# Entry to the first stage, set-up transfers, order of the modulation vectors and the compressed branch of a two-block transformer kernel

## Chip, cores and metric

The kernel runs on one core of one Trainium2 chip. The metric is the device time of one execution in microseconds (us), as the median of several runs. The core has a matrix engine (TensorE, PE in the rows; PEld is its weight load), a vector engine (DVE), a scalar engine (ACT), GpSimd (POOL) and SyncE, whose queue (SP) issues nearly all transfers.

## Reference

Two transformer blocks, each with two layers, run one after the other over 256 tokens of width 1024, all in float32. The first block's layer is feed-forward, mixing (retention, block attention, convolution), feed-forward. The second block's layer has the same shape with a modulation, computed from one vector `c`:

```
cond = silu(c)
for l in range(2):
    mod = cond @ ada_w[l] + ada_b[l]          # 9 vectors of 1024
    sh1, sc1, ga1, sh2, sc2, ga2, sh3, sc3, ga3 = split(mod, 9)
    n = rms_norm(h) * (1 + sc1) + sh1 ; h = h + 0.5 * ga1 * swiglu(n)
    n = rms_norm(h) * (1 + sc2) + sh2 ; h = h + ga2 * token_mixing(n)
    n = rms_norm(h) * (1 + sc3) + sh3 ; h = h + 0.5 * ga3 * swiglu(n)
```

Inside `token_mixing` one of three attentions has a compressed branch: 15 overlapping windows of 32 keys (and of 32 values) are each flattened and sent through a small two-layer network.

```
def compress(t, j):                            # j = 0 keys, 1 values
    blk = t[:, cmp_idx] + cmp_pe[j]            # 15 windows x 32 x 64
    hid = silu(blk.reshape(15, 2048) @ cmp_w1[j])   # 128 wide
    return hid @ cmp_w2[j]
```

## The kernel before

The program is twelve stages in a row (`SUBS`): f1, m, f2 twice for the first block, F1, M, F2 twice for the second. The same Python class hierarchy is played once per engine, so every engine's instructions are written in one common order; semaphores do the rest.

**Weights.** All weights stream from memory in units of up to 1 MB through four buffers `raw`. A unit is cut into subs of two 128-row tiles of 512 columns. For each sub ACT writes a rounded copy `wh` (`split_hi`, L2021) and DVE the remainder `wl` (`split_lo`, L2292); PE then does three matmuls per tile and half of the tokens: `xh*wh`, `xh*wl`, `xl*wh` (`sub`, L1713, L1714, L1716), twelve in a full sub. There are five `wh`/`wl` buffers, and `ahead` keeps the splits three subs in front of PE in feed-forward stages. SyncE issues the load of a buffer's next unit behind the remainder of its last sub (`load`, L2747).

**Entry.** `enter` turns `x` (2 x 128 tokens by 1024) with sixteen PE transposes (L1688) into banks 6 and 7: eight, then eight more in the same two banks once ACT (`xh`, L2048) and DVE (`xl`, L2339) have read the first eight. Only behind all of this come the first three weight splits (`ahead`), and behind them the four squares of the norm (L2041).

**Set-up.** Behind the first four weight loads SyncE issues 18 transfers of constants: the large part of `cst` (1.7 MB), convolution weights, embeddings, positions, `w2d`, `lngb`. In the second column chunk of the first stage (`c == 1`), right behind `turn_h(0)`, `setup_rest` has PE turn three small tiles one behind the other, and DVE and ACT compute the rotary angles.

**Modulation.** The 36 vectors of 512 columns (`q`; 72 half units of weights) are summed by DVE: one multiply-add over 128 x 512 per weight tile (`mac`, L2300), four to a half unit. `ADA_BY` says how many half units are placed by the end of each stage from the fourth on. When a vector is whole, ACT and DVE split it (`ach`, `acl`), PE sums it over the partitions with two matmuls (`sum_mod`, L1739, L1740), and `keep_mod` stores it: shift and scale as columns `shc`, `Gc`, gates as rows `gaB`. Vectors are taken in the order of stage `s` and part `i` (0, 1 shift; 2, 3 scale; 4, 5 gate).

**Compressed branch.** In stage M, `cmp_hidden` (L1929) runs 16 float32 matmuls for the keys and, one sub (`fill`) later, 16 for the values. The 15 windows are the stationary side, the 128 columns of `w1b` the moving side; both write partitions 0 to 14 of a bank. Each such matmul is two records in the trace. ACT takes the silu (L2204), PE turns it, ACT copies it to `small` (L2210).

Of the kernel before, what the change touches and what calls it, by code (L numbers as in the profile page):

```python
# [88 lines left out]
ADA_BY = [8, 8, 20, 32, 32, 50, 68, 68, 72]  # L89
# [14 lines left out]
class Weights:  # L104
# [41 lines left out]
    def ada(self, upto, a, b):  # L146
        n = upto - self.ada_at
        for m in range(n):
            q, half = divmod(self.ada_at, 2)
            s, i = divmod(q, 6)  # L150
# [50 lines left out]
class Memory:  # L201


    def __init__(self, nc, ctx):
# [37 lines left out]
        self.shc = [sb(f"shc{i}", [P, 8]) for i in range(2)]  # L242
        self.Gc = [sb(f"Gc{i}", [P, 8]) for i in range(2)]
# [133 lines left out]
class Order:  # L377
# [5 lines left out]
    def __init__(self, k, e, count):  # L383
# [12 lines left out]
        self.rt_free, self.gab_free, self.col_free = None, [None, None], [None, None]  # L396
        self.jobs, self.posts = [], []
        self.foxb_free, self.x_sum = None, None
        self.set_up = False
# [142 lines left out]
    def reduce_one(self):  # L542
        q, _ = self.reduces.pop(0)
        s, i = divmod(q, 6)
# [44 lines left out]
    def setup_rest(self):  # L589
        b = [self.next_t() for _ in range(3)]  # L590
        self.setup_parts(b)
        for i, n in enumerate(("cols2", "cols3", "posf")):
            self.free[b[i]] = (self.s.vec, n)

    def setup_parts(self, b):
        pass
# [120 lines left out]
    def shifted_lo(self, s, t, p):  # L717
# [4 lines left out]
        self.col_free[s % 2] = done  # L722
# [132 lines left out]
    def ffn(self, label, s, nx):  # L855
# [18 lines left out]
        for c in range(6):  # L874
            if c < 5:
# [9 lines left out]
                if c == 1 and not self.set_up:  # L885
                    self.set_up = True
                    self.setup_rest()
                k = 0
                while k < 8:
                    n, tu = self.gemm_sub(label + "u", bu, self.k.X, k, 8, self.XW)  # L890
                    k += n
                    if k == FK:
                        self.flush(1)
                w = 512
# [449 lines left out]
    def mix2(self, l, a, nx):  # L1344
# [53 lines left out]
        def fv_done(b, tk):  # L1398
# [9 lines left out]
            def post():  # L1408
                b = self.next_t()
                self.fox_sums(l, b)  # L1410
                self.free[b] = rdy["cq"]
# [42 lines left out]

        for kv in range(2):
            b = self.next_t()
            self.cmp_hidden(l, kv, b)
            self.ptT_free[kv] = (s.prod, ("cmp1", l, kv))
            w1_free.append((s.prod, ("cmp1", l, kv)))
            self.free[b] = (s.act, ("hid", l, kv))  # L1460
            self.fill()
        b = self.next_t()
        self.cmp_turn(l, b)
        self.free[b] = (s.act, ("hidT", l))
# [144 lines left out]
    def cmp_hidden(self, l, kv, b):  # L1609
        pass  # L1610

    def cmp_turn(self, l, b):
# [34 lines left out]
    def run(self):  # L1647
# [5 lines left out]
        self.free[5] = (self.s.vec, "cols1")  # L1653
# [27 lines left out]
class Tensor(Order):  # L1681
# [13 lines left out]
    def setup_parts(self, b):  # L1695
        m, s = self.m, self.s
        self.wait_ge((s.rows2, 112), self.free[b[0]])
        self.then_inc(self.transpose(m.ps[b[0]][:, 0:128], m.rows2[:, :]), (s.turned, "rows2"))
        self.wait_ge(self.free[b[1]])
        self.then_inc(self.transpose(m.ps[b[1]][:, 0:64], m.rows3[0:64, :]), (s.turned, "rows3"))  # L1700
        self.wait_ge((s.vec, "posr"), (s.vec, "cols2"))
        self.then_inc(self.transpose(m.ps[b[2]][:, 0:2], m.posr[0:2, :]), (s.turned, "pos"))
# [220 lines left out]
    def cmp_hidden(self, l, kv, b):  # L1923
        m = self.m
        blk = m.ptT[kv][:, 0:240].rearrange("p (j n) -> p j n", j=16)
        w1 = m.w1b[kv][:, :].rearrange("p (j n) -> p j n", n=128)
        self.wait_ge((self.s.w1[kv], 16 * (l + 1)), (self.s.vec, ("blk", l, kv)), self.free[b])
# [4 lines left out]
    def cmp_turn(self, l, b):  # L1932
# [919 lines left out]
```

## Time and profile before

| | |
|---|---|
| median of 3 runs | 2259.04 us (2258.34 to 2262.61) |
| the profiled execution's own time | 2256.14 us |
| its span, first to last instruction | 2254.3 us |
| PE busy | 2219.8 us, 98% of the span |
| DVE busy | 1522.8 us, 68% |
| ACT busy | 1160.8 us, 51% |
| share of the chain that ended last: PE, DVE, DMA, ACT | 87%, 7%, 3%, 2% |
| bytes moved | 462.94 MB, mean 205 GB/s |

The profile is one execution. A matmul's record is longer than its share of the stream, since matmuls are pipelined: what a stretch of PE costs is read from start to start. Busy shares are averages over twelve stages with different limits. The difference between the execution's time and its span is 1.84 us.

### The profile page before, as it was taken

The page shows a single profiled execution, that of the slowest core. Times are in us where ns is not written, and L with a number is a line of the kernel's source. Part 1 is how long each engine was busy: PE and PEld are TensorE (multiplying, and loading weights), DVE is VectorE, ACT ScalarE, POOL GpSimd, SP SyncE. Part 2 cuts the span into 40 slices and gives each one's busy share as a digit, 9 for nine tenths or more (in the row PEclk, how much of TensorE's full clock was granted, in tenths as well). Part 3 has the DMA queues.
Part 4 walks back from the last instruction along what each step waited for, and adds up shares of the span by engine and source line. Part 5 has one row for each costly group of instructions (what it writes and reads, how often), then busy time and mean ns, then how long its engine had stood idle before and what let it go on. Part 6 is the DMA issues. An engine that isn't in the chain of part 4 may idle for free.

```text
span 2254.3 us, 27255 instructions
## 1 busy us (share of the span) xinstructions
PE 2219.8 (98%) x10956; PEld 1874.1 (83%) x10956; DVE 1522.8 (68%) x2299; ACT 1160.8 (51%) x1803; POOL 51.6 (2%) x46
## 2 busy tenths in 40 slices
PE   7999999999999999999999999999999999999998
PEld 6888988888888988878888988888888889888887
DVE  4555975556776967857885545799689955457664
ACT  4544654444445655444445556644454455566443
POOL 0000000000000000010001000100000010001000
PEclk9999999999999999999999999999999999999999
DMA  7554555556765557865776444588779864445653
GB/s 272 187 196 151 158 171 176 187 198 213 235 231 164 159 174 277 282 215 198 266 264 185 141 134 146 190 301 296 261 244 320 289 189 136 136 143 180 233 196 122
DMA packets 250642, 462.94 MB, mean 205 GB/s; under 512 B 9798, under 2 KB 55792, under 8 KB 250388
## 3 DMA queue, kind: packets, MB, share of 16 engines
q1 hardware_dynamic: 250276, 461.04, 60.4%
q8 instruction: 86, 1.41, 0.3%
q14 instruction: 40, 0.33, 0.0%
q10 hardware_dynamic: 240, 0.16, 0.0%
HBM read 460.12 MB, written 1.05 MB: 205 GB/s over the span
## 4 chain that ended last, share of the span: by engine, by line
PE 87%; DVE 7%; DMA 3%; ACT 2%; issue 1%; POOL 0%; ACTq 0%; SPq 0%; DVEq 0%; POOLq 0%
PE ps L1713 18%; PE ps L1716 17%; PE ps L1714 17%; PE s L1716 7%; PE s L1713 7%; PE s L1714 7%; PE ps L1688 4%; DVE wl L2292 2%; PE ps L1852 1%; DMA raw<-in_ffn_w_out 1%; PE s L1832 1%; DMA raw<-in_ffn_w_in 1%; PE ps L1729 1%; PE ps L1727 1%; PE ps L1728 1%
## 5 line engine op out<-in xcount | busy, mean ns | idle before, releaser
L2292 DVE TENSOR_TENSOR wl<-raw,wh 128x1024 fp32r<-128x1024 f32 (+2 forms) x732 | 850.5, 1181 | 263.3 <-ACT wh L2021 258.9
L2021 ACT ACTIVATE wh<-raw 128x1024 fp32r<-128x1024 f32 (+2 forms) x744 | 750.6, 1026 | 530.1 <-PE ps L1716 261.3
L1713 PE MATMUL ps<-wh,xh 128*128 128x512 f32 (+3 forms) x1632 | 622.2, 381 | 3.4 <-DVE wl L2292 3.4
L1716 PE MATMUL ps<-wh,xl 128*128 128x512 f32 (+3 forms) x1632 | 610.6, 374 | 0.0
L1714 PE MATMUL ps<-wl,xh 128*128 128x512 f32 (+3 forms) x1632 | 609.8, 374 | 0.0
L1713 PEld LDWEIGHTS ps<-wh,xh 128*128 128x128 f32 x1632 | 307.1, 188 | 57.0 <-issue 8.2
L1716 PEld LDWEIGHTS ps<-wh,xl 128*128 128x128 f32 x1632 | 306.8, 188 | 47.3
L1714 PEld LDWEIGHTS ps<-wl,xh 128*128 128x128 f32 x1632 | 307.4, 188 | 44.8
L2300 DVE SCALAR_TENSOR_TENSOR acc<-raw,condT,acc 128x512 f32<-128x512 f32 x252 | 188.7, 749 | 5.1
L1713 PE MATMUL s<-wh,xh 128*128 128x512 f32 x384 | 150.1, 391 | 0.0
L1716 PE MATMUL s<-wh,xl 128*128 128x512 f32 x384 | 149.6, 389 | 0.0
L1714 PE MATMUL s<-wl,xh 128*128 128x512 f32 x384 | 149.5, 389 | 0.0
L1713 PE MATMUL s<-wh,hTh 128*128 128x512 f32 x352 | 138.6, 394 | 0.0
L1716 PE MATMUL s<-wh,hTl 128*128 128x512 f32 x352 | 137.3, 390 | 0.0
L1714 PE MATMUL s<-wl,hTh 128*128 128x512 f32 x352 | 137.1, 389 | 0.0
L2399 DVE TENSOR_TENSOR hTl<-ps,hTh 128x512 fp32r<-128x512 f32 x88 | 57.0, 686 | 98.6 <-ACT hTh L2088 98.6
L2088 ACT ACTIVATE hTh<-ps 128x512 fp32r<-128x512 f32 x88 | 48.2, 595 | 136.5 <-PE ps L1688 136.5
L1713 PE MATMUL ps<-wh,hTh 128*128 128x512 f32 x268 | 104.5, 390 | 0.0
L1716 PE MATMUL ps<-wh,hTl 128*128 128x512 f32 x268 | 104.3, 389 | 0.0
L1714 PE MATMUL ps<-wl,hTh 128*128 128x512 f32 x268 | 104.3, 389 | 0.0
L2041 ACT ACTIVATE junk<-x 128x512 f32<-128x512 f32 x56 | 35.5, 634 | 96.1 <-DVE x L2379 60.3
L1716 PEld LDWEIGHTS s<-wh,xl 128*128 128x128 f32 x384 | 72.1, 188 | 15.1
(330 smaller groups left out, 2586.6 us busy)
## 6 DMA issues: line engine op xcount, KB each, us to landing
raw<-in_ffn_w_in SPq DMA_DIRECT2D x80, 1024.0 KB, 5.3
raw<-in_ada_w SPq DMA_DIRECT2D x72, 1024.0 KB, 6.5
raw<-in_ffn_wg SPq DMA_DIRECT2D x40, 1024.0 KB, 5.4
raw<-in_ffn_wu SPq DMA_DIRECT2D x40, 1024.0 KB, 5.3
raw<-in_ffn_wd SPq DMA_DIRECT2D x40, 1024.0 KB, 5.4
raw<-in_ffn_w_out SPq DMA_DIRECT2D x40, 1024.0 KB, 6.6
raw<-in_mix_w_in SPq DMA_DIRECT2D x28, 1024.0 KB, 5.1
raw<-in_w_in SPq DMA_DIRECT2D x28, 768.0 KB, 4.5
```

Source lines behind the costliest of these rows:

```text
L1688: return self.e.transpose(out, src, self.m.ident[0:n, 0:n])
L1713: e.matmul(o, X[0](kk, t), hi, start=kk == 0, stop=False)
L1714: e.matmul(o, X[0](kk, t), lo, start=False, stop=False)
L1716: ins = e.matmul(o, X[1](kk, t), hi, start=False, stop=kk == K - 1)
L1727: e.matmul(o, X[0](kk, t), hi, start=kk == 0, stop=False)
L1728: e.matmul(o, X[0](kk, t), lo, start=False, stop=False)
L2021: ins = self.e.activation(m.wh[j % NH][:, 0:n], m.raw[u % NR][:, k0 * w:k0 * w + n], ACT.Copy)
L2041: self.then_inc(self.e.activation(m.junk[:, :], m.x[:, t, h * 512:(h + 1) * 512], ACT.Square, scale=1.0 / 32, accum_out=m.ssq[:, 2 * h + t ...
L2088: self.then_inc(self.e.activation(m.hTh[:, k:k + 2, :].rearrange("p k s -> p (k s)"), m.ps[b], ACT.Copy), th)
L2292: ins = self.e.tensor_tensor(m.wl[j % NH][:, 0:n], m.raw[u % NR][:, k0 * w:k0 * w + n], hi, ALU.subtract)
L2300: ins = self.e.scalar_tensor_tensor(out=a, in0=m.raw[u % NR][:, k * 512:k * 512 + 512], scalar=m.condT[:, kk:kk + 1], in1=a if kk else m.b ...
L2399: self.then_inc(self.e.tensor_tensor(lo, m.ps[b], hi.bitcast(F32), ALU.subtract), tl)
```

## The change

It has five parts.

1. Entry: the sixteen transposes go to four banks (6, 7, 2, 3) without a wait between the halves, and each pair of tiles is followed by one weight split. A dummy ACT instruction on a blank element of `junk` stands ahead of everything, so that the table of functions is loaded there.
2. Set-up turns: the three small transposes are set behind the second and third sub of the second chunk's up half and behind the second sub of the third chunk's; the angles follow behind one sub more.
3. Set-up transfers: instead of 18 in a row, one behind each of the first 18 subs; the large `cst` part is the eighth.
4. Modulation: `ADA_BY` moves half units between stages, the gate vectors of stage s come behind shift and scale of stage s+1, and `shc`, `Gc` have three buffers. Half units per feed-forward stage, before: 0, 0, 8, 12, 12, 18, 18, 4; now: 0, 0, 14, 13, 13, 14, 14, 4.
5. Compressed branch: the 32 matmuls are issued in turns, keys, values, keys, values; the values' output goes to partitions 32 to 46 of another bank. There is one `fill` fewer in front of the attention and so one more behind it. The forget gate's sums take bank 6.

```diff
-ADA_BY = [8, 8, 20, 32, 32, 50, 68, 68, 72]
+ADA_BY = [14, 14, 27, 40, 40, 54, 68, 68, 72]
+ADA_SEQ = [(s, i) for s, gate in ((0, 0), (1, 0), (0, 1), (2, 0), (1, 1), (3, 0), (2, 1), (4, 0), (3, 1), (5, 0), (4, 1), (5, 1))
+           for i in (range(4, 6) if gate else range(4))]
...
     def enter(self, nx):
-        self.prep(0, nx)
-        self.prep(1, nx)
-        self.ahead()
+        for n, p in enumerate(self.prep_turn(0, (6, 7)) + self.prep_turn(1, (2, 3))):
+            self.prep_hi([p], nx)
+            self.prep_lo([p], nx)
+            self.ahead(min(n + 1, 3), 0)
...
+    def setup_more(self):
+        if self.transfers < 18:
+            self.setup_load(self.transfers)
+            self.transfers += 1
...
-                if c == 1 and not self.set_up:
-                    self.set_up = True
-                    self.setup_rest()
                 k = 0
                 while k < 8:
                     n, tu = self.gemm_sub(label + "u", bu, self.k.X, k, 8, self.XW)
                     k += n
+                    self.setup_more()
                     if k == FK:
                         self.flush(1)
+                    if k in (4, 6) and not self.set_up:
+                        if c == 1:
+                            self.setup_rest(k // 2 - 2)
+                        elif c == 2 and k == 4:
+                            self.setup_rest(2)
+                        elif c == 2:
+                            self.angles()
+                            self.set_up = True
...
-        for kv in range(2):
-            b = self.next_t()
-            self.cmp_hidden(l, kv, b)
...
+        bb = (self.next_t(), self.next_t())
+        self.cmp_hidden(l, bb)
...
         for j in range(16):
-            ins = self.e.matmul(m.ps[b][0:15, 0:P], blk[:, j, :], w1[:, j, :], start=j == 0, stop=j == 15)
-        self.then_inc(ins, (self.s.prod, ("cmp1", l, kv)))
+            for kv in range(2):
+                ins = self.e.matmul(m.ps[bb[kv]][32 * kv:32 * kv + 15, 0:P], blk[kv][:, j, :], w1[kv][:, j, :],
+                                    start=j == 0, stop=j == 15)
+        self.then_inc(ins, (self.s.prod, ("cmp1", l)))
...
+        self.wait_ge((s.vec, "blank"))
+        self.then_inc(e.activation(m.junk[:, 1:2], m.junk[:, 0:1], ACT.Copy), (s.act, "tables"))
```

**ACT at the entry.** Before, from its first table load to the fourth weight split: eight `xh`, three splits (`wh`), four squares.

```order
L2048 ACT_TABLE_LOAD
L2048 ACTIVATE xh<-ps,cols_67 128x256 x8
L2021 ACTIVATE wh_57<-raw_53 128x1024
L2021 ACTIVATE wh_58<-raw_53 128x1024
L2021 ACTIVATE wh_59<-raw_54 128x1024
L2041 ACTIVATE junk,ssq<-x 128x512 x4
L2021 ACTIVATE wh_60<-raw_54 128x1024
```

Now, the same place:

```order
L2038 ACT_TABLE_LOAD
L2038 ACTIVATE junk<-junk 128x1
L2081 ACTIVATE xh<-ps,cols_67 128x256 x2
L2054 ACTIVATE wh_57<-raw_53 128x1024
L2081 ACTIVATE xh<-ps,cols_67 128x256 x2
L2054 ACTIVATE wh_58<-raw_53 128x1024
L2081 ACTIVATE xh<-ps,cols_67 128x256 x2
L2054 ACTIVATE wh_59<-raw_54 128x1024
L2081 ACTIVATE xh<-ps,cols_67 128x256 x2
L2074 ACTIVATE junk,ssq<-x 128x512 x4
L2054 ACTIVATE wh_60<-raw_54 128x1024
```

The first split stands behind two `xh` instead of eight, and DVE's `xl` and `wl` alternate in the same way.

**PE in the compressed branch of the first stage M.** Before, the end of a sub, the keys' chain, a sub (its first and last rows), the values' chain:

```order
L1716 MATMUL ps<-wh_61,xl 128x384
L1929 MATMUL ps<-w1b_130,ptT_107 15x128 x16
L1713 MATMUL ps<-wh_57,xh 128x384
...
L1716 MATMUL ps<-wh_57,xl 128x384
L1929 MATMUL ps<-w1b_131,ptT_108 15x128 x16
L1713 MATMUL ps<-wh_58,xh 128x384
```

Now there are 32 rows in turns, of which these are the first four and the last:

```order
L1741 MATMUL ps<-wh_61,xl 128x384
L1957 MATMUL ps<-w1b_132,ptT_109 15x128
L1957 MATMUL ps<-w1b_133,ptT_110 15x128
L1957 MATMUL ps<-w1b_132,ptT_109 15x128
L1957 MATMUL ps<-w1b_133,ptT_110 15x128
...
L1957 MATMUL ps<-w1b_133,ptT_110 15x128
L1738 MATMUL ps<-wh_57,xh 128x384
```

The number of matmuls is the same; the sub that stood between the chains now stands behind both.

**PE at the first set-up turn.** Before, the three small transposes stand in a row between the transposes of the hidden tile `hb` and the next matmul:

```order
L1688 MATMUL ps<-cst,hb_92 128x128
L1688 MATMUL ps<-cst,rows_150 128x128
L1688 MATMUL ps<-cst,rows_151 128x64
L1688 MATMUL ps<-cst,posr 128x2
L1713 MATMUL ps<-wh_59,xh 128x512
```

Now each stands between two matmuls of the stream; here the first:

```order
L1738 MATMUL ps<-wh_60,xh 128x512
L1739 MATMUL ps<-wl_65,xh 128x512
L1741 MATMUL ps<-wh_60,xl 128x512
L1711 MATMUL ps<-cst,rows_152 128x128
L1738 MATMUL ps<-wh_61,xh 128x512
```

Two subs have been set between the hidden tile's transposes and the first of the three.

## Rows read from the trace of the kernel before

**Rows 1.** PE's waits over the whole span: us in total, times, longest us.

```profile
PE ps L1739 <- DVE acl L2307: 2.1, 3, 1.2
```

**Rows 2.** Timeline of the entry: start us, us, engine, line, operation, tiles, idle before it.

```profile
7.30 1.91 PE L1688 MATMUL ps<-cst,x 128*128 128x128 f32 x8
7.89 1.28 ACT L2048 ACT_TABLE_LOAD   x1 [7.89 <-DVE cols L2250]
9.19 1.57 ACT L2048 ACTIVATE xh<-ps,cols 128x256 fp32r<-128x256 f32 x4
10.06 1.66 DVE L2339 SCALAR_TENSOR_TENSOR xl<-ps,cols,xh 128x256 fp32r<-128x256 f32 x4 [2.25 <-ACT xh L2048]
10.99 2.32 PE L1688 MATMUL ps<-cst,x 128*128 128x128 f32 x8 [1.78 <-DVE xl L2339]
...
14.37 2.96 ACT L2021 ACTIVATE wh<-raw 128x1024 fp32r<-128x1024 f32 x3
15.47 3.50 DVE L2292 TENSOR_TENSOR wl<-raw,wh 128x1024 fp32r<-128x1024 f32 x3
...
16.75 0.80 PE L1713 MATMUL ps<-wh,xh 128*128 128x512 f32 x1 [3.44 <-DVE wl L2292]
...
17.34 0.63 PE L1714 MATMUL ps<-wl,xh 128*128 128x512 f32 x1
...
17.77 0.63 PE L1716 MATMUL ps<-wh,xl 128*128 128x512 f32 x1
...
21.33 0.39 PE L1714 MATMUL ps<-wl,xh 128*128 128x512 f32 x1
...
21.56 0.39 PE L1716 MATMUL ps<-wh,xl 128*128 128x512 f32 x1
```

**Rows 3.** The first weight loads (tile raw, issues from 2 to 4 us).

```profile
L2747 SPq DMA_DIRECT2D raw<-in_ffn_wg x2: 409/450/492, 2.6 to 3.1; - x2
DMA to landing us min/median/max: 7.0/9.3/11.4
```

**Rows 4.** Timeline at the set-up turns.

```profile
51.04 1.04 PE L1688 MATMUL ps<-cst,hb 128*128 128x128 f32 x8
...
53.14 0.30 PE L1688 MATMUL ps<-cst,rows 128*128 128x128 f32 x1 [1.07 <-DVE hTl L2399]
...
54.51 0.49 PE L1713 MATMUL ps<-wh,xh 128*128 128x512 f32 x1
```

**Rows 5.** Windows: length; busy us (count) of PE, PEld, DVE, ACT, POOL; clock, DMA share, GB/s.

```profile
510.00:699.00 189.00, 188.65 (x862) 156.37 (x860) 129.20 (x149) 88.10 (x109) 0.70 (x1) 1.00 0.67 224
1003.00:1205.00 202.00, 196.95 (x890) 162.65 (x889) 146.09 (x185) 97.56 (x136) 8.47 (x7) 0.98 0.66 229
1435.00:1631.60 196.60, 195.13 (x898) 161.06 (x897) 164.23 (x210) 98.37 (x134) 8.01 (x6) 1.00 0.79 273
1000.00:1050.00 50.00, 44.95 (x199) 36.47 (x198) 28.95 (x47) 25.59 (x47) 7.05 (x6) 0.93 0.45 155
```

**Rows 6.** Timeline of SyncE's queue: set-up transfers.

```profile
9.08 9.10 SPq L2723 DMA_DIRECT2D rows<-in_conv_w  x4
...
21.73 1.30 SPq L2729 DMA_DIRECT2D w2d<-in_nsa_cmp_w  x3
```

**Rows 7.** The first window of rows 5, multiply-adds of the modulation (L2300) alone.

```profile
510.00:699.00 189.00, 23.96 (x32) 1.00 0.67 224
```

**Rows 8.** Timeline of PE in the second stage F1.

```profile
1791.97 0.50 PE L1739 MATMUL ps<-ach,onesr 128*128 128x512 f32 x1 [1.16 <-DVE acl L2307]
```

**Rows 9.** Timeline of PE in the first stage M: the keys' chain.

```profile
1234.71 3.67 PE L1929 MATMUL ps<-w1b,ptT 128*15 128x128 f32 x32
```

**Rows 10.** PE groups by shape, 1200 to 1420 us: count | busy us, mean ns | idle.

```profile
L1929 PE MATMUL ps<-w1b,ptT 128*15 128x128 f32 x64 | 7.3, 273 | 0.0
...
L1832 PE MATMUL s<-Tdk,Tdq 64*128 64x256 f32 x12 | 3.1, 393 | 0.0
...
L1832 PE MATMUL s<-Tfk,Tfq 64*128 64x256 f32 x12 | 1.8, 377 | 0.0
```

More of the change, by code:

```diff
@@ L241, in __init__ @@
         self.bt = [sb(f"bt{i}", [P, 512]) for i in range(2)]
-        self.shc = [sb(f"shc{i}", [P, 8]) for i in range(2)]
-        self.Gc = [sb(f"Gc{i}", [P, 8]) for i in range(2)]
+        self.shc = [sb(f"shc{i}", [P, 8]) for i in range(3)]
+        self.Gc = [sb(f"Gc{i}", [P, 8]) for i in range(3)]
         self.ssq = sb("ssq", [P, 4])
@@ L587, in begin, with setup_rest, setup_part, setup_load @@
         pass
[L589 to L595, printed above, removed]
+    def setup_rest(self, i):
+        b = self.next_t()
+        self.setup_part(i, b)
+        self.free[b] = (self.s.vec, ("cols2", "cols3", "posf")[i])
+    def setup_part(self, i, b):
+        pass
+    def setup_more(self):
+        if self.transfers < 18:
+            self.setup_load(self.transfers)
+            self.transfers += 1
+    def setup_load(self, i):
+        pass
+    def angles(self):
         pass
@@ L1607, in cmp_blocks, with cmp_hidden, cmp_turn @@
         pass
[L1609 removed]
+    def cmp_hidden(self, l, bb):
         pass
[L1612 removed]
+    def cmp_turn(self, l, bb):
         pass
@@ L1693, in begin, with setup_part @@
         self.then_inc(self.transpose(m.ps[5][:, 0:104], m.rows1[0:104, :]), (s.turned, "rows1"))
-    def setup_parts(self, b):
+    def setup_part(self, i, b):
         m, s = self.m, self.s
[L1697 to L1702, printed above, removed]
+        self.wait_ge(self.free[b], (s.rows2, 112))
+        if i == 0:
+            self.then_inc(self.transpose(m.ps[b][:, 0:128], m.rows2[:, :]), (s.turned, "rows2"))
+        elif i == 1:
+            self.then_inc(self.transpose(m.ps[b][:, 0:64], m.rows3[0:64, :]), (s.turned, "rows3"))
+        else:
+            self.wait_ge((s.vec, "posr"))
+            self.then_inc(self.transpose(m.ps[b][:, 0:2], m.posr[0:2, :]), (s.turned, "pos"))
     def sub(self, j, hs, nk, w, banks, X, kpos, K, ready):
@@ L2052, in shifted @@
         m = self.m
-        return self.e.activation(out, ps, ACT.Identity, scale=m.Gc[s % 2][:, k:k + 1], bias=m.shc[s % 2][:, k:k + 1])
+        return self.e.activation(out, ps, ACT.Identity, scale=m.Gc[s % 3][:, k:k + 1], bias=m.shc[s % 3][:, k:k + 1])
     def shifted_v_part(self, s, t, p, b, o, tk):
@@ L2199, in fox_forget, with cmp_hidden, cmp_turn @@
         self.then_inc(e.activation(ab, ab, ACT.Ln, bias=1.0), (s.act, ("flog", l)))
-    def cmp_hidden(self, l, kv, b):
+    def cmp_hidden(self, l, bb):
         m = self.m
-        self.wait_ge((self.s.prod, ("cmp1", l, kv)), self.pt_free[kv])
-        self.then_inc(self.e.activation(m.pt[kv][0:15, 512:640], m.ps[b][0:15, 0:P], ACT.Silu), (self.s.act, ("hid", l, kv)))
-    def cmp_turn(self, l, b):
+        for kv in range(2):
+            r = slice(32 * kv, 32 * kv + 15)
+            self.wait_ge((self.s.prod, ("cmp1", l)), self.pt_free[kv])
+            self.then_inc(self.e.activation(m.pt[kv][r, 512:640], m.ps[bb[kv]][r, 0:P], ACT.Silu), (self.s.act, ("hid", l, kv)))
+    def cmp_turn(self, l, bb):
         m = self.m
-        hid = m.small[:, 128:192].rearrange("p (v n) -> p v n", v=2)
         self.wait_ge((self.s.turned, ("hidT", l)))
-        self.then_inc(self.e.activation(hid[:, :, 0:15], m.ps[b][:, 0:32].rearrange("p (v n) -> p v n", v=2)[:, :, 0:15],
-                                        ACT.Copy), (self.s.act, ("hidT", l)))
+        for kv in range(2):
+            self.then_inc(self.e.activation(m.small[:, 128 + 32 * kv:143 + 32 * kv], m.ps[bb[kv]][:, 0:15], ACT.Copy),
+                          (self.s.act, ("hidT", l, kv)))
     def cmp_scores(self, l, qn):
```

128 lines of the change are left out of this document (72 added, 56 removed).

## The prediction

> **What bounds the kernel now.** I read the page first: PE is busy 98% of the span and makes 87% of the chain that ended last, so time can only come from PE: matmuls that get cheaper, stretches in which it stands still, and stretches in which it runs slowly. Then PE's list of waits. Past the first 7 us, in which the first constants arrive, it holds few large ones. One belongs to the modulation: 2.1 us in three waits, the longest 1.2, for `acl` [rows 1]. The rest is at the entry, at the set-up turns and at the change of blocks, so I read the timeline in the first two.
>
> At the entry, PE turns eight tiles from 7.30, waits 1.78 us for its two banks, turns eight more from 10.99, waits 3.44 us for the first `wl` and begins the stream at 16.75 [rows 2]. The reader is to see ACT in the same rows: a table load of 1.28 us, eight `xh` in two lots, and only at 14.37 the first weight split, though the first weights had landed 7.0 us after their issue at 2.6, by 9.6 [rows 3]. From then on PE has no wait until 53.14, where a set-up turn stands 1.07 us behind `hTl` [rows 4].
>
> **Clock.** Matmuls of 512 columns start 0.43 us apart at 17.34 and 17.77, and 0.23 apart at 21.33 and 21.56 [rows 2]: the 1.2 GHz level for about the first 3 us after the stream begins, then the 2.4 GHz level. Where PE stood still at the change of blocks the granted clock of the window falls to 0.93 [rows 5]. The change doesn't touch that place. It makes executions differ: the profiled one took 2256.14 us, 2.9 less than the median of 2259.04.
>
> **The change part by part.**
>
> *Entry.* PE's transposes take about 0.24 us each at most (1.91 / 8), so the first pair of tiles, whole with the sixth, is there at 7.30 + 6 x 0.24 = 8.8. The table is loaded before that, since ACT has nothing else to do. Two `xh` at 0.39 (1.57 / 4): 9.6, the same moment at which the first weights have landed [rows 2, 3]. One split 0.99 (2.96 / 3): 10.6; `wl` starts 0.1 behind it, as 15.47 stands behind 14.37 + 0.99, and takes 1.17 to 1.24: 11.9 to 12.0. DVE's two `xl` (0.42 each) are over by 10.5. PE starts at about 12.05 instead of 16.75: **4.7 us** less. Does it then run dry? The second `wl` comes after two more `xl`: 12.0 + 0.83 + 1.17 = 14.0; the third at 16.0. The first sub's twelve matmuls need 12.05 to about 16 with the slow stretch of 3 us, the second ends at 18.8. Both are in time. The fourth split stands behind the squares and ACT's last `xh`; PE wants it at about 21.5, six us after the third. The bounds: if the first sub waited for the second buffer of weights as well, or the slow stretch got longer by 3 us, 1.5 would be lost; if the sixteen transposes without a pause bring the clock up earlier, up to 1.5 (half of the slow stretch) is won. So 3.2 to 6.2.
>
> *Set-up turns.* From the first `hb` transpose to the next matmul 54.51 - 51.04 = 3.47 us pass, of which the eight transposes take at most 1.04: 2.4 us for three tiny turns [rows 4]. Two subs (24 matmuls at 0.23, 5.4 us) now lie between `turn_h` and the first of them, so the wait on `hTl` is covered. What is left is the turns themselves, at most 0.30 each, 0.9 together: **1.6 us** less, between 1.1 (the one wait alone) and 2.2. Without that cover it would be the 1.07 again. The angles' short DVE and ACT work is moved, not added; three subs of splits stand ahead of PE and hide it.
>
> *Set-up transfers.* Eighteen issues are moved past weight loads in SyncE's queue. In an idle queue one takes 0.43 us (1.30 / 3); behind the first loads four took 9.10, 2.3 each [rows 6]. A sub takes 2.7 us, so even at 2.3 each plus one weight load in two subs the queue keeps up. `rows2` is issued behind the seventh sub and used behind the fourteenth. I take 0 from it.
>
> *Modulation.* The number of vectors stays; 0.75 us of DVE per multiply-add (23.96 / 32) makes 3.0 us per half unit [rows 7]. The two stages with 18 half units have DVE at 164 of 197 us and a DMA share of 0.79; they fall by 4, 12 us, to 152. The stage with 8 goes to 14: 129.2 + 18 = 147 of 189, about where the stage at 1003 is today, with 146 of 202 [rows 5]. The longest of the three `acl` waits, 1.16 us at 1791.97, lies in the second of the two full stages [rows 8]. Of the 2.1 us I count **1.5** as gone; bounds -2.6 and, if the newly loaded stage gets the same waits, 0.
>
> *Compressed branch.* The keys' chain occupies PE for 3.67 us from 1234.71, 32 records at 0.11 each [rows 9]; both take 7.3 us of PE [rows 10]. Each uses 15 of the array's columns. If two matmuls in different columns run side by side as pairs, 32 pairs take about the time of one chain: 3.7 us plus 0.1, so 3.5 less per layer, **7.0** for both. No row of before shows pairs by columns. The nearest rows are pairs by rows of the array: the twelve 64x256 records of `Tfk,Tfq`, which alternate two heads in the two halves of the rows, take 1.8 us, the twelve of `Tdk,Tdq`, issued one head at a time, 3.1 us [rows 10], the ratio 0.58 with the pipeline's tail in it. So the bounds are 7.0 won and 0; I take 7.0, since a matmul's time here is its stream of 128 columns and both kinds of pair leave cells of their own to each stream. On the way in, both blocks of windows must be ready 6 us earlier for the values; they are made by DVE right behind each other.
>
> A rule speaks against it. The Trainium skill ("TensorE: Matmul & The Clock Gate", Part 3) says that a weight load overlaps with matmuls in flight only when its row group differs; here both chains use all rows, and by that rule the pairs would follow each other: 7.8 us instead of 14.8. The same section of the skill also gives a speedup of 2.38 for three tiles by columns with 512 moving columns, by which they would overlap. No row here shows either.
>
> *The rest of stage M.* One sub moves behind the attention, two small ACT copies replace one, four ACT passes over `gts` fall away: ACT is at half load there. 0.
>
> **Sum**: 4.7 + 1.6 + 1.5 + 7.0 = 14.8 us. The profiled execution would take 2256.1 - 14.8 = 2241.3 (span 2239.5), the median 2259.0 - 14.8 = **2244.2**.
>
> **Rivals.**
> 1. *The chains don't overlap.* Both use all rows of the array, so that each weight load may have to wait for the other chain's matmul; the pairs stay at 0.11 us per record, and 4.7 + 1.6 + 1.5 = 7.8 us remain: 2251.2. For it: no row shows pairs by columns. Against: the pairs by rows. 20%. (This is what the skill's rule, named above, would give.)
> 2. *The entry moves no further than the weights.* If with sixteen transposes and the interleaving ACT, DVE and PE trade short waits, or the slow stretch of the clock repeats, the entry gives 2.5 rather than 4.7, and the modulation nothing: 2244.2 + 2.2 + 1.5 = 2247.9. The rows speak against a long wait; ACT and the landing meet at 9.6 within 0.1 us. 12%.
> 3. *Slower: each turn between column groups waits out the previous matmul.* A chain record lasts 273 ns from start to end [rows 10]. If PE drained before each change of columns, 64 records would take 64 x 0.273 = 17.5 us instead of 7.3 per layer, 10.2 more, 20.4 for both: with the 7.8 of the rest, 12.6 slower, 2271.6. It decides from 0.175 us per record on ((7.3 + 3.9) / 64), and is beyond the measurement from 0.21. Against it: the pairs by rows change groups each time too and cost less. 2%.
> 4. *The change does little.* Overlap missing and the entry and modulation giving under 4.5 together with the turns: above 2254.5. 4%.
>
> **How the numbers follow.** The sum holds with 62%, by itself 2240 to 2247.5: the bounds above are hardly met together. The range goes down to all upper bounds at once, 6.2 + 2.2 + 2.6 + 7.0 = 18.0, with the scatter of the runs 2239.5, and up to the first rival with its entry 1 us short, 2252. Changes of under 0.2% (4.5 us) can't be told from none here. Faster by more: 62 + 20 + 12 = 0.94; within 0.04; slower 0.02.
>
> **What would show it.** In the changed kernel's timeline the first stream matmul stands at 12.0 (11.6 to 13.5), with no wait in the 16 transposes. Between the last `hb` transpose near 47 and the next matmul there is no turn, and later turns cost 0.3 each. In stage M, 64 records of `w1b` lie in 3.7 us, starts some ns and 0.11 us apart in turn; 7.3 would be rival 1, 17 rival 3. `acl` waits are under 0.6 us in all, with DVE near 147 us in the stage now given 14 half units instead of 8. I'd be wrong through the columns first, and second through a PE wait that appears in a stage of the first block where there is none now.

## The result

The changed kernel takes **2237.26 us** in the median (four executions, 2236.9 to 2238.68); the kernel before took 2258.69 beside it (2255.46 to 2262.61). The ratio is 0.9906 with the interval [0.9888, 0.9923]: 21.4 us less, where 14.8 were forecast. The direction was as forecast, and the time lies 2.2 us below the low end of the range.

The profiled execution of the changed kernel took 2237.55 us, with a span of 2235.7. Its page, busy time and the chain that ended last:

```profile
span 2235.7 us, 27260 instructions
PE 2208.3 (99%) x10956; PEld 1867.3 (84%) x10956; DVE 1523.6 (68%) x2300; ACT 1157.1 (52%) x1802; POOL 51.6 (2%) x46
PE 94%; DVE 4%; ACT 1%; issue 0%; DMA 0%; POOL 0%; SPq 0%; DVEq 0%; POOLq 0%; ACTq 0%
```

PE was 87% of the chain and is 94%: what has gone is mostly other engines' time on the chain, and PE's own busy time fell from 2219.8 to 2208.3. Its waits over the whole span (us in total, times, longest us):

```profile
PE s L1711 <- DMA rows<-in_ffn_norm: 7.1, 1, 7.1
PE ps L1817 <- DVE xl L2405: 2.9, 1, 2.9
PE ps L1784 <- DVE dg L2387: 2.6, 3, 2.0
PE ps L1738 <- DVE wl L2332: 1.4, 1, 1.4
PE ps L1798 <- ACT xh L2105: 1.3, 6, 0.2
PE ps L1711 <- ACT ym L2144: 1.2, 1, 1.2
```

The waits for `acl` [rows 1] are gone. The wait for `ym L2144` is new. Now the entry, by the timeline, against [rows 2]:

```profile
2.81 1.28 ACT L2038 ACT_TABLE_LOAD   x1 [2.81 <-issue]
...
7.35 3.62 PE L1711 MATMUL ps<-cst,x 128*128 128x128 f32 x16
...
8.88 0.84 ACT L2081 ACTIVATE xh<-ps,cols 128x256 fp32r<-128x256 f32 x2 [4.57 <-PE ps L1711]
...
10.02 1.06 ACT L2054 ACTIVATE wh<-raw 128x1024 fp32r<-128x1024 f32 x1 [0.31 <-DMA raw<-in_ffn_wg]
...
11.11 1.22 DVE L2332 TENSOR_TENSOR wl<-raw,wh 128x1024 fp32r<-128x1024 f32 x1 [0.49 <-ACT wh L2054]
...
12.39 0.79 PE L1738 MATMUL ps<-wh,xh 128*128 128x512 f32 x1 [1.42 <-DVE wl L2332]
```

The sixteen transposes run without a wait and the stream starts at 12.39 instead of 16.75, 4.4 us earlier. The first split waits 0.31 us for the landing of the first weights and starts at 10.02, where the forecast had both ready at 9.6.

At the set-up turns ([rows 4]) PE has no wait. From the first `hb` transpose to the stream's next matmul 0.79 us pass, where it was 3.47, and the first turn stands between two matmuls of the stream:

```profile
46.66 1.03 PE L1711 MATMUL ps<-cst,hb 128*128 128x128 f32 x8
47.45 0.48 PE L1738 MATMUL ps<-wh,xh 128*128 128x512 f32 x1
...
52.99 0.27 PE L1711 MATMUL ps<-cst,rows 128*128 128x128 f32 x1
53.02 0.47 PE L1738 MATMUL ps<-wh,xh 128*128 128x512 f32 x1
```

The modulation's stages, by the windows that answer to [rows 5] (length; busy us and count of PE, PEld, DVE, ACT, POOL; clock, DMA share, GB/s):

```profile
506.00:695.00 189.00, 188.65 (x861) 156.37 (x860) 151.25 (x182) 88.25 (x109) 0.70 (x1) 1.00 0.74 257
999.00:1201.00 202.00, 196.52 (x894) 161.84 (x893) 151.27 (x194) 97.86 (x137) 8.46 (x7) 0.99 0.69 235
1427.00:1619.30 192.30, 192.08 (x882) 159.34 (x883) 149.71 (x188) 95.59 (x129) 6.29 (x5) 1.00 0.75 257
```

DVE is now at about 150 us in all three. The third window is shorter also because its ends were chosen anew. From the stage's first `dg` row to the next stage's first, the stage takes 1619.3 - 1427.0 = 192.3 us where it took 1630.6 - 1435.8 = 194.8: 2.5 less. About 1.0 of that is not won: two of its nine sums over the partitions, 0.5 us each, now stand in other stages. Of the chains in the first stage M, against [rows 9], one row is left, with twice the records in the same time:

```profile
1230.73 3.67 PE L1957 MATMUL ps<-w1b,ptT 128*15 128x128 f32 x64
```

**Stage M by landmarks.** From the last `dg` row ahead of the stage to the first `ym` row behind its attention it takes 1391.09 - 1209.73 = 181.36 us before and 1382.27 - 1205.78 = 176.49 after: 4.87 less, where 3.5 were forecast. The second stage M gives 4.83. And in the first block's second stage m there is a wait that the kernel before doesn't have:

```profile
767.97 1.55 PE L1877 MATMUL ps<-mv,ptT 128*128 128x64 f32 x12
770.69 0.63 PE L1711 MATMUL ps<-cst,cacc 128*128 128x128 f32 x4 [1.17 <-ACT ym L2144]
```

The two profiled executions differ by 18.6 us, the medians by 21.4. So two questions stood: why stage M is 4.87 us shorter and not 3.5, and where the 2.8 us lie that the two traces do not show.

### The profile page after: what moved, and what is told of

Read it like the earlier page. It is cut to its first block, busy times and chain, and to the rows that moved or that the text cites. A ratio compares the mean times of both kernels' runs of the same rounds, so it can differ in the third digit from the quotient of the medians.

```text
span 2235.7 us, 27260 instructions
## 1 busy us (share of the span) xinstructions
PE 2208.3 (99%) x10956; PEld 1867.3 (84%) x10956; DVE 1523.6 (68%) x2300; ACT 1157.1 (52%) x1802; POOL 51.6 (2%) x46
## 4 chain that ended last, share of the span: by engine, by line
PE 94%; DVE 4%; ACT 1%; issue 0%; DMA 0%; POOL 0%; SPq 0%; DVEq 0%; POOLq 0%; ACTq 0%
PE ps L1738 19%; PE ps L1741 19%; PE ps L1739 19%; PE s L1741 7%; PE s L1738 7%; PE s L1739 7%; PE ps L1711 4%; PE ps L1877 2%; PE s L1857 1%; DVE wl L2332 1%; PE ps L1754 1%; PE ps L1752 1%; PE ps L1753 1%; PE ps L1784 1%; DVE gts L2693 1%; PE ps L1817 1%
## 5 line engine op out<-in xcount | busy, mean ns | idle before, releaser
L1739 PEld LDWEIGHTS s<-wl,xh 128*128 128x128 f32 x384 | 72.1, 188 | 14.8
```

Of the source, the lines that this page charges most:

```text
L1739: e.matmul(o, X[0](kk, t), lo, start=False, stop=False)
```

## The experiments

Each kernel was timed in up to five rounds beside the kernel before, on one chip for each group. The edits are shown in part. Differences are of medians within a group, unless a trace is named.

**First group: one part at a time, on top of the kernel before** (before: 2258.46).

*Compressed branch alone*, with the chains' pairs, the two turns and `fox_sums` in bank 6:

```diff
-                b = self.next_t()
-                self.fox_sums(l, b)
-                self.free[b] = rdy["cq"]
+                self.fox_sums(l, 6)
+                self.free[6] = rdy["cq"]
...
+        bb = (self.next_t(), self.next_t())
+        self.cmp_hidden(l, bb)
```

> The kernel before with the compressed branch's edit alone (both chains in column pairs, two turns in two banks, fox_sums in bank 6). Theory A (the branch's edit takes away more than the pairs: also the switches between blocks of small matmuls and the stream that fall away, one chain's way in and out, and the wait before fox_sums): each of the two stages M is 4.8 us shorter, 9.7 together, about 2249.0 by the median. Rival B (only the pairs are the edit's own, the rest came through the modulation's or the entry's part): 3.4 per stage, 6.8 together, about 2251.9.

Measured: 2248.08, 10.4 us less, ratio 0.9953 [0.9940, 0.9965]. By its trace each stage M is 4.8 us shorter, so theory A holds.

*Modulation alone* (`ADA_BY`, `ADA_SEQ`, three buffers).

```diff
-ADA_BY = [8, 8, 20, 32, 32, 50, 68, 68, 72]
+ADA_BY = [14, 14, 27, 40, 40, 54, 68, 68, 72]
```

> The kernel before with the modulation's order alone (half units per stage, sequence, third buffers). Theory A (the part is worth what the trace shows in the stages at 1003 to 1830, less the new wait of 1.17 us before the convolution's turn in layer 1, and it takes the scatter as well): 2.6 us in the profile and up to 5.4 by the median, 2253.3 to 2256.1, with executions within 3 us of each other. Rival B (the scatter of 7 us between executions of the kernel before belongs to another place): 2.6 us at most and the scatter stays at 5 to 7 us. Rival C (the part wins nothing by itself, its gain is eaten by the new wait): within 1 us of before.

Measured: 2257.12, 1.3 us less, ratio 0.9994 [0.9985, 1.0002]. The part wins little and can't be told from nothing by itself: its trace has no `acl` wait, and it has the new wait of 1.17 us. The gain is nearer rival C's than A's, but of the scatter theory A is right: the eleven executions lie within 1.0 us, though the old set-up turns are still in them. Kernels with the old order and as many executions or more scatter more widely: the kernel before over 8.5 us (29 executions), the one with the entry alone 10.0 (12), those with the turns moved 5.8 and 5.1 (11 each). So the scatter of the kernel before goes with the order of the modulation and not with the turns.

The traces show a place for it. From the last `hb` transposes of the second stage F1, near 1767, to the first `dg` row of the next stage all ten traces with the new order take 55.88 us. The seven with the old one take 57.77 in the kernel before, the least of them, and up to 61.03. One sum of 0.5 us that has moved is in that; the rest are `acl` waits, and in the two slowest a slow stretch behind them. In the trace with bank 6 for `fox_sums` (last group) it begins like this, the granted clock of 1792 to 1799 us being 0.76:

```profile
1793.87 0.54 PE L1738 MATMUL ps<-ach,onesr 128*128 128x512 f32 x1 [2.11 <-DVE acl L2306]
...
1794.64 0.63 PE L1712 MATMUL s<-wh,hTh 128*128 128x512 f32 x1
1795.06 0.63 PE L1713 MATMUL s<-wl,hTh 128*128 128x512 f32 x1
```

*Entry alone*:

```diff
-        self.prep(0, nx)
-        self.prep(1, nx)
-        self.ahead()
+        for n, p in enumerate(self.prep_turn(0, (6, 7)) + self.prep_turn(1, (2, 3))):
+            self.prep_hi([p], nx)
+            self.prep_lo([p], nx)
+            self.ahead(min(n + 1, 3), 0)
```

> The kernel before with the entry alone (sixteen transposes in a row, tiles split two by two, first weight split between them, table loaded early). Theory A: first stream matmul at 12.4 us, 4.4 us less in all, 2254.3. Rival B (the early start meets slower arrivals later in the first subs, and half is given back): 2.2 us less, 2256.5.

Measured: 2253.33, 5.1 us less, ratio 0.9982 [0.9973, 0.9991], with executions from 2250.6 to 2260.6. The stream starts at 12.05, but PE later waits once for a weight split that it didn't wait for before, so that its trace is ahead by 2.7 us at 48 us, not by 4.7. PE's waits in its first 80 us, in part:

```profile
PE ps L1690 <- DVE hTl L2405: 1.3, 2, 1.1
PE s L1715 <- DVE wl L2298: 1.2, 1, 1.2
PE ps L1715 <- DVE wl L2298: 1.0, 1, 1.0
```

The 1.2 for the tile `s` is the new one, at 35.7 us; the 1.0 is the first of the stream. The gain of the medians is rather theory A's, the place of the loss is B's; the interval, 2 to 6 us, holds both.

*Set-up turns and transfers alone*, the turns between the later subs and the transfers one behind each sub:

```diff
-                if c == 1 and not self.set_up:
-                    self.set_up = True
-                    self.setup_rest()
...
+                    self.setup_more()
...
+                    if k in (4, 6) and not self.set_up:
+                        if c == 1:
+                            self.setup_rest(k // 2 - 2)
```

> The kernel before with the set-up turns between later subs and the set-up transfers one behind each sub. Theory A: 1.8 us less, 2256.9, no wait of PE at the turns, and nothing from the transfers. Rival B (the transfers among the first weight loads matter: without them the first weights land earlier): the first stream matmul is more than 0.5 us earlier and the gain is over 2.5 us.

Measured: 2254.56, 3.9 us less, ratio 0.9985 [0.9976, 0.9993], though its stream starts at 16.79 as before. Neither theory: the gain is that of rival B, the mechanism isn't. The four parts together make 10.4 + 1.3 + 5.1 + 3.9 = 20.7 of the 21.4: they add up, though the interval of each is 2 to 3 us to either side.

**What the traces of this group showed.** The kernel with the compressed branch alone lost time against the profiled kernel before in a place that it does not touch. After the pause at the old set-up turns its matmuls start 0.43 us apart for a while (the 1.2 GHz level). Its timeline there:

```profile
54.26 0.30 PE L1688 MATMUL ps<-cst,rows 128*128 128x128 f32 x1 [1.07 <-DVE hTl L2406]
54.77 0.27 PE L1688 MATMUL ps<-cst,rows 64*128 64x64 f32 x1 [0.20 <-DVE hTl L2406]
55.48 0.22 PE L1688 MATMUL ps<-cst,posr 2*128 2x2 f32 x1 [0.44 <-DVE posr L2266]
...
57.64 0.63 PE L1713 MATMUL ps<-wh,xh 128*128 128x512 f32 x1
58.07 0.63 PE L1714 MATMUL ps<-wl,xh 128*128 128x512 f32 x1
58.50 0.63 PE L1716 MATMUL ps<-wh,xl 128*128 128x512 f32 x1
```

Its window, ...

```profile
54.00:60.00 6.00, 5.10 (x15) 3.90 (x16) 4.98 (x19) 2.09 (x4) 0.00 (x0) 0.72 0.00 0
```

... and the same one of the kernel before:

```profile
54.00:60.00 6.00, 5.64 (x25) 4.72 (x26) 5.13 (x17) 3.21 (x5) 0.00 (x0) 1.00 0.00 1
```

The waits are the same; the granted clock is 0.72 in the one and 1.00 in the other. So the profiled execution on which the forecast rests happened to be one in which this pause had no consequence. The programs are the same up to this place, so the difference is one between executions.

**Second group: on top of the changed kernel.** The changed kernel once more, as the mark:

> The changed kernel once more, as the mark for the three kernels beside it and for its own scatter. Theory A (what made the kernel before differ between executions is the clock after the pause at the set-up turns, which this kernel no longer has): 2237.3, with executions within 3 us of each other. Rival B (the narrow spread of four executions was luck): a spread of 5 us or more.

Measured: 2236.63 (2235.79 to 2239.1); before 2257.9. In this trace the stream has no slow stretch at the entry at all: its first matmul records take 0.50 and 0.39 us, where the first trace's take 0.79 and 0.63, and it is 1.8 us ahead of that one from there on. The four executions lie within 3.3 us, between what A and B wanted. What A gives as the cause of the old scatter does not hold: by the kernel with the modulation alone it is the modulation's order.

*Bank 6 for the convolution's turn.*

```diff
+                self.tbank = 7
                 b = self.next_t()
                 self.conv_turn(l, b, tok)
```

> The changed kernel with bank 6 instead of 7 for the convolution's turn, in both layers. Theory A (the wait of 1.17 us at 770 comes from the odd number of reductions in the stage ahead, which turns the alternation of the two banks round, so that the transposes meet the bank that the last retention values still hold): the wait is gone and the kernel is 1.15 us faster, 2236.1. Rival B (the transposes must wait for ym for another reason, or the next step waits instead): the 1.15 us show up again within the stage, no change.

Measured: 2234.05, 2.6 us under the mark, ratio to before 0.9894 [0.9881, 0.9908]. The wait for `ym L2144` is gone from the list. Against the mark its trace wins 1.3 us in that stage, and no wait takes its place: theory A. The gain by medians was larger than the wait, which the last group takes up.

*Both chains in the same columns*, the silu and the turns reading partitions 0 to 14 to match, all else as changed:

```diff
-                ins = self.e.matmul(m.ps[bb[kv]][32 * kv:32 * kv + 15, 0:P], blk[kv][:, j, :], w1[kv][:, j, :],
+                ins = self.e.matmul(m.ps[bb[kv]][0:15, 0:P], blk[kv][:, j, :], w1[kv][:, j, :],
```

> The changed kernel with both chains in the same columns (partitions 0 to 14 of two banks, still in turns, same order of everything). Theory A (the pairs run side by side because they stand in different columns; the rest of what stage M won is the order's): 64 records 0.11 us apart, 7.0 us instead of 3.67, each stage M 3.4 us longer, 2244.1. Rival B (two banks and the turns are enough for overlap): no change, 2237.3. Rival C (all 4.8 us of the stage come with the columns): 9.7 longer, 2247.

Measured: 2243.96, 7.3 us over the mark, ratio to before 0.9938 [0.9925, 0.9952]. Between the landmarks of stage M it takes 3.60 us more than the first trace of the changed kernel in the first stage and 3.59 in the second. The 64 records in its timeline:

```profile
1230.58 7.16 PE L1957 MATMUL ps<-w1b,ptT 128*15 128x128 f32 x64
```

Banks, turns and order are the same in both; 32 columns' distance halves the time. Theory A.

*Set-up transfers at the start again:*

```diff
     def setup_more(self):
-
-        if self.transfers < 18:
-            self.setup_load(self.transfers)
-            self.transfers += 1
+        pass
...
         for u in range(NR):
             self.load(u, None)
+        for i in (7, *range(7), *range(8, 18)):
+            self.setup_load(i)
```

> The changed kernel with the eighteen set-up transfers issued at the start again, behind the first weights. Theory A (with the early entry PE meets a late weight unit, as the kernel with the entry alone did at 35.7): a wait of PE for wl of 1.2 us near 36, 1.2 us longer, 2238.5; more, up to 3, if the clock falls behind it. Rival B (the transfers are hidden, as forecast): no change.

Measured: 2240.59, 4.0 us over the mark, executions 2238.8 to 2244.3. PE stands 2.47 us before a weight split, and a slow stretch follows:

```profile
36.97 0.50 PE L1735 MATMUL s<-wh,xh 128*128 128x512 f32 x1 [2.47 <-DVE wl L2329]
...
38.67 0.63 PE L1735 MATMUL s<-wh,xh 128*128 128x512 f32 x1
39.10 0.63 PE L1736 MATMUL s<-wl,xh 128*128 128x512 f32 x1
```

The cause stands in SyncE's queue: the set-up transfers occupy it from 6 us on, and the next weights are issued only at 27.48. ACT then waits 11.7 us for them, up to 34.61.

```profile
9.11 9.48 SPq L2763 DMA_DIRECT2D rows<-in_conv_w  x4
18.63 2.39 SPq L2765 DMA_DIRECT2D rows<-in_conv_b  x1
...
27.48 0.98 SPq L2795 DMA_DIRECT2D raw<-in_ffn_wg  x2
```

In the mark the same two loads are issued from 13.97 on:

```profile
13.97 6.42 SPq L2796 DMA_DIRECT2D raw<-in_ffn_wg  x2
```

So theory A, with more than its upper price. How much of it is the queue's order and how much the bandwidth that the large `cst` transfer takes is not separated.

**Third group: turns and transfers apart, and the order in stage M** (before: 2260.14; the changed kernel was not run on this chip, so the second two are read against the mark's distance to before on another, 21.3).

*The kernel before with the turns moved, transfers at the start:* the edit of the turns above without `setup_more`.

> The kernel before with the set-up turns between later subs, and the set-up transfers at the start as before. Theory A (the pause of PE at the old turns costs its own 1.8 us and, in most executions, a slow stretch of the clock of 1.5 to 1.9 us behind it; the transfers give nothing while the entry is late): 3.5 us less, 2254.5, as the kernel with both. Rival B (the turns are worth their 1.8 us, the other 2 us belong to the transfers): 2256.3.

Measured: 2257.04, 3.1 us less, ratio 0.9988 [0.9979, 0.9996]. That is nearer theory A's 3.5, but the interval, 0.9 to 4.7 us, holds both. The traces decide. From the kernel's first block of `hb` transposes to its third, traces with the turns in one place take 48.0 us without a slow stretch (two) or 49.6 to 49.7 with one (five), and those with moved turns 46.2 to 46.3 (ten). So the turns are worth 1.8 us or 3.4, by whether the stretch comes.

*The kernel before with the transfers moved, turns in their old place:*

```diff
                 if c == 1 and not self.set_up:
                     self.set_up = True
-                    self.setup_rest()
+                    for i in range(3):
+                        self.setup_rest(i)
+                    self.angles()
...
+                    self.setup_more()
```

> The kernel before with the set-up transfers one behind each sub, and the turns in their old place. Theory A: nothing, 2258 within 0.7 us. Rival B (the transfers hold the weights up in the first 40 us): 2 us less, 2256.

Measured: 2259.95, 0.2 us less, ratio 1.0001 [0.9992, 1.0010]. So with the late entry the transfers are worth nothing that could be measured, and theory A holds. Its trace has `acl` waits of 4.6 us, where [rows 1] has 2.1: these waits too differ from execution to execution.

*The changed kernel with the turns back in one place:*

```diff
+                if c == 1 and not self.set_up:
+                    self.set_up = True
+                    for i in range(3):
+                        self.setup_rest(i)
+                    self.angles()
```

> The changed kernel with the set-up turns back in one place before the second chunk. Theory A (clock behind the pause): a slow stretch of 7 to 9 matmuls near 52 in more than half of the executions, 3.5 us slower in the middle, 2240.1, and executions 4 us and more apart. Rival B (the pause costs only itself): 2238.4 and within 3 us.

Measured: 2242.04, 18.1 under before: 3.2 less than the changed kernel wins, so 3.2 lost. Its window around the turns, with seven slow matmuls in it:

```profile
47.00:53.00 6.00, 5.21 (x17) 4.11 (x17) 4.87 (x18) 2.46 (x5) 0.00 (x0) 0.72 0.00 0
```

From its `hb` transposes at 44.69 to those at 71.61 pass 26.92 us, in the changed kernel 69.88 - 46.66 = 23.22. Of the 3.7 between them 2.1 are the turns and their pause (51.04 to 76.39 in the kernel before is 25.35, 2.13 more than 23.22), and 1.6 the clock; 0.35 comes back in the next chunk, where the third turn no longer stands. The size is theory A's; its executions lie within 2.6 us, so that the spread of 4 us that A wanted isn't there. The stretch may come in nearly all of its executions, which one trace can't show.

*One sub more between the chains and their turns*, so that the subs stand where they stood before:

```diff
         self.fill()
+        self.fill()
         bb = (self.next_t(), self.next_t())
         self.cmp_turn(l, bb)
```

> The changed kernel with one sub more between the compressed branch's chains and its turns, so that the subs behind it stand where they stood in the kernel before. Theory A (1.2 us of each stage M came from this order: small blocks of matmuls stand next to each other, and fox_sums finds its input ready): stage M 0.8 us longer each, as the chain's way in and out stays saved, 2238.3. Rival B (the 1.2 us belong to the chains and to the bank of fox_sums alone): within 0.3 us per stage, 2236.9.

Measured: 2237.8, 22.3 under before, no loss. Between the landmarks each stage M is 0.27 and 0.25 us longer than in the first trace of the changed kernel: rival B. The order of the subs is a small part of the 1.4 us. This trace also has a slow stretch behind the wait at 770, the granted clock of the 6 us from 768 being 0.72.

**Fourth group: the last two open points** (before: 2259.25).

*The kernel before with bank 6 for `fox_sums`*, two lines:

> The kernel before with bank 6 for fox_sums alone. Theory A (the wait before fox_sums, 0.5 us in most traces and 1.7 in one, is for bank 7, which the attention's values hold, and this one line takes it away): no wait of PE before the logf matmuls, 0.6 us less per stage M, 1.2 together and some tenths more for the clock, some 1.5 us under the kernel before beside it. Rival B (the wait is for logf itself, and went through the order of the subs): the wait stays and the time too.

Measured: 2256.28, 3.0 us less, ratio 0.9989 [0.9981, 0.9998]. Its waits in the two stages M and what lies between:

```profile
PE ps L1738 <- DVE acl L2306: 2.1, 1, 2.1
PE ps L1772 <- ACT xh L2071: 0.9, 4, 0.2
PE ps L1758 <- DVE dg L2346: 0.3, 1, 0.3
```

In the kernel before the same stretch has a wait for `ym` ahead of the sums, which are queued behind it in order:

```profile
1312.57 0.36 PE L1918 MATMUL ps<-logf,cst 128*128 128x6 f32 x2 [0.46 <-DVE ym L2427]
```

With the bank alone changed it is gone, and the stages M are 0.68 and 0.53 us shorter: theory A for the mechanism. Of the 3.0 us by medians (interval 0.5 to 4.3) the trace shows 1.2; the rest is not shown. The sums need nothing of `ym`; they needed bank 7, from which DVE was still reading the attention's values. In the trace with the turns moved and the transfers at the start this wait was once 1.7 us and a slow stretch of seven matmuls followed, 3.1 us in that stage.

*The changed kernel and bank 6 for the convolution's turn, side by side:*

> The changed kernel as a mark beside the next one: 2236.6 to 2237.3.

> The kernel with bank 6 for the convolution's turn again, beside the changed one. Theory A (the wait of 1.17 us is followed by a slow stretch of the clock in some executions, as one trace showed it): 2.0 to 2.6 us under the changed kernel. Rival B (the wait costs only itself and the first comparison was helped by the scatter): 1.2 us under it.

Measured: 2238.36 (ratio to before 0.9909 [0.9895, 0.9923]) and 2235.5 (0.9896 [0.9880, 0.9911]), 2.9 us apart. In the trace of the first the wait is followed by a slow stretch:

```profile
770.64 0.78 PE L1711 MATMUL ps<-cst,cacc 128*128 128x128 f32 x4 [1.17 <-ACT ym L2144]
771.36 1.65 PE L1920 MATMUL s<-Trq,Trk 64*128 64x256 f32 x8
...
773.43 0.52 PE L1739 MATMUL ps<-wl,xh 128*128 128x384 f32 x1
```

Eight records take 1.65 us here and 0.92 in the first trace of the same kernel, behind the same wait of 1.17. Of the eight traces that have this wait, two have the slow stretch, and it costs 1.5 us there. Two in eight are too few to make 1.2 us into 2.6 and 2.9. The traces show a second place, the change of blocks: from its first `dg` row to the next `hb` transposes both traces with bank 6 take 42.2 us and all three of the changed kernel 43.4. But of two other kernels whose code is the changed kernel's up to there one takes 43.4 as well and the other 44.6, so whether the 1.2 us belongs to the bank is not shown. The time is: over both groups bank 6 gives 2.6 and 2.9 us, and it is the version that beats both kernels, 24 us under the kernel before.

## Why the forecast missed

The step that failed is the term "the rest of stage M ... 0": it was worth 2.5 us in the two stages. Beside it the set-up turns were mis-sized, 1.6 us where 3.1 and 3.2 were measured, because the slow stretch behind their pause was left out. Point by point, by the forecast's own terms:

- **Entry, 4.7 (3.2 to 6.2).** Right in size, but only together with the transfers: 5.1 alone by medians, 4.4 in the first trace, 6.2 in the second. In the eight traces that have the new entry and no transfers at the start, the kernel's first `hb` transposes stand 4.4 to 6.4 us earlier than in the profiled kernel before; in the two that have the transfers at the start, 2.7 and 1.4. The upper bound, half or more of the slow stretch won, was the part to watch: of ten traces with the new entry five have no slow stretch behind it, of seven with the old one none is without (7 to 14 matmuls at 0.20 us more each, 1.4 to 2.8 us, by the spacings 0.43 and 0.23).
- **Set-up turns, 1.6 (1.1 to 2.2).** Mis-sized: 3.1 and 3.2 in the two experiments that isolate them. (By its own terms the sum was 2.4 - 0.9 = 1.5.) The 1.8 that the two first traces differ by there was forecast; that the pause also brings the clock down behind it was not, because [rows 4] come from an execution in which it did not. Of seven traces with the turns in one place five have the slow stretch behind them; the ten with moved turns have none there.
- **Set-up transfers, 0.** Right for the late entry (0.2 measured) and wrong in this change, where 4.0 are lost without it. The forecast asked whether PE runs dry in the first three subs, and not what the earlier stream wants of the weights behind the 18 issues. It belongs to the entry: without it the entry has a wait of 1.2 to 2.5 us near 36 us. So the sum was not hurt by it, only its division.
- **Modulation, 1.5 (0 to 2.6).** In the range: 1.3 alone, which can't be told from nothing, and no row of before shows the 2.6. What the forecast did not see is that its 2.1 us of waits were those of a good execution. The `acl` waits are gone in all ten traces that have the new order and there in all seven that haven't, 1.2 to 4.6 us. The new wait for `ym` gives 1.2 or more of it back. The forecast had named such a wait, in a stage of the first block, as the second thing that could be wrong; its cause is shown by the bank's kernel. Seven reductions instead of four in the stage ahead turn the alternation of banks 6 and 7 round, so the convolution's turn meets the bank of the values.
- **Compressed branch, 7.0 (0 to 7.0).** Right in its mechanism, and a bound that wasn't one. The pairs by columns run side by side: 3.6 us per stage against 3.5. By the rule cited in the forecast (the Trainium skill, "TensorE: Matmul & The Clock Gate", Part 3), they should have followed each other; here the measurement decides, 64 records in 3.67 us with all rows in use by both. What the forecast cited against that rule from the same section, a speedup by columns, is what the runs bear out.
- **"The rest of stage M ... 0".** This step failed. By the traces it is worth 1.3 us per stage: the wait for bank 7 ahead of `fox_sums` 0.6 (one line of the diff, read as a detail), the chain's way into and out of the stream once instead of twice about 0.4 (what is left of the 4.87, not measured by itself), and the order of the subs 0.26. By medians the branch gives 10.4.

**The numbers together.** 10.4 - 7.0 = 3.4 for the branch, some 1.5 to 2.3 for the clock behind the turns, and 0.4 for the entry, less 0.2 for the modulation, bring the sum of 14.8 to 19.9 to 20.7 of the 21.4. The range's low end was the sum of the upper bounds, 18.0, and 1.5 for scatter, and two of these bounds were too low: the turns' took a wait at its length, and the branch's held the pairs and nothing else. The forecast's rows also came from a lucky execution, and that answers where most of the 2.8 us between the two differences lies: it took 2256.14 us where the median beside the changed kernel is 2258.69. It is the fastest of the seven traces with the old parts at the entry (its first `hb` transposes at 51.04, the others with the old entry at 51.18 to 52.41) and near 1767 (57.77 against 57.84 to 61.03), and one of two in seven without a slow stretch behind the turns. Rivals 1 to 4 are all out: the chains overlap, the entry moves as far as it should, and no change of column group costs a drain.

What isn't shown: why a pause is followed by a slow stretch in one execution and not in the next. The traces only count the cases, and each kernel has one trace, the changed one three and the one with bank 6 two.

## What to carry to other kernels

When the engine that bounds the kernel pauses for a microsecond or more, price the pause at its length plus the slow stretch that may follow, and look for that in several traces: one trace can show either. Where work alternates between two buffers or banks, follow the alternation through the change: a wait named for some far-off result may be for the bank it leaves, and a different count of uses in front moves it to another place. When a stream is made to start earlier, check what its later supplies are queued behind, not only the first.

## What the runs showed of the hardware

- Two chains of float32 matmuls with 128 moving columns and 15 stationary ones, both over all 128 rows, run side by side when their outputs lie in different column groups (partitions 0 to 14 and 32 to 46): 3.67 us for 64 records, 7.16 in one group.
- Behind pauses of PE of 1.1 to 2.9 us matmuls ran at the 1.2 GHz level for a while (5 to 8 starts 0.43 us apart for 512 columns, granted clock of such a window of 6 or 7 us 0.72 to 0.76) in some executions and not in others: two of eight traces behind a wait of 1.17 us, with one of three of the same program among them, and five of seven behind the set-up turns.
- Sixteen transposes without a pause ahead of the stream left no slow stretch behind the entry in five of ten traces; two lots of eight with waits between them left one in all seven. There the stretch is told by the starts, 0.43 us apart and not 0.23; the profile's granted clock says 1.00 there (16 to 24 us in the kernel before, 12 to 16 in the changed one).
